# A seven-product 2x2 block form for the down projections of a two-layer decoder step, with the hidden rows in three parts

## The reference

```
h  = rmsnorm(x)                         # 1032 x 1024
u  = h @ W_up                           # 1024 -> 2 * 2816, float32
u  = u[t-2]*w[0] + u[t-1]*w[1] + u[t]*w[2]   # causal, per column, with a saved state
z  = silu(u[:, :2816]) * u[:, 2816:]
x  = x + z @ W_down                     # 2816 -> 1024
```

## Time and profile before

| | us |
|---|---|
| median of 3 runs | 2892.84 |
| the profiled execution: span | 2890.9 |
| PE busy | 2675.3 |
| DVE busy | 1348.3 |
| ACT busy | 1153.7 |
| POOL busy | 468.1 |
| up tiles 1 to 43 of layer 0 | 451.50 |
| down tiles 0 to 6 of layer 0 | 202.32 |

### The profile page before, as it was taken

The page is one execution under the profiler, slowest core; times in us unless marked ns, Lnnn a source line. Parts: engine busy times, 40 slices in busy tenths (PEclk is TensorE's granted clock), DMA queues, the critical chain, the costliest instruction groups (busy, mean ns, idle before and its releaser), DMA issues.

```text
span 2890.9 us, 47469 instructions
## 1 busy us (share of the span) xinstructions
PE 2675.3 (93%) x18103; PEld 1816.1 (63%) x18103; DVE 1348.3 (47%) x2199; ACT 1153.7 (40%) x1599; POOL 468.1 (16%) x626
## 2 busy tenths in 40 slices
PE   5898988898888798999999999999999999999997
PEld 3666676655565465666666665566655666666664
DVE  8254454315899736444444113522345444443123
ACT  4665655322777624444443112211124444442111
POOL 0321303313445300111111000011100111111000
PEclk9999999999999899999999999999999999999999
DMA  3222223364000211111112111111111111111111
GB/s 129 82 74 61 66 68 118 95 188 129 1 1 1 81 51 37 51 45 49 51 51 66 51 51 35 51 51 51 47 42 44 51 51 51 51 51 66 50 50 59
DMA packets 113484, 173.20 MB, mean 60 GB/s; under 512 B 16993, under 2 KB 83922, under 8 KB 112978
## 3 DMA queue, kind: packets, MB, share of 16 engines
q1 hardware_dynamic: 92610, 150.90, 16.2%
q0 software_dynamic: 3792, 12.58, 1.3%
q10 hardware_dynamic: 16960, 8.16, 1.0%
HBM read 161.47 MB, written 14.30 MB: 61 GB/s over the span
## 4 chain that ended last, share of the span: by engine, by line
PE 74%; DVE 14%; ACT 5%; SPq 3%; issue 3%; DMA 1%; POOL 0%; ACTq 0%; DVEq 0%; POOLq 0%
PE PS L1804 62%; ACT xT L855 2%; DVE R L1552 2%; SPq L554 2%; PE PS L1784 2%; DVE R L1222 2%; PE PS L1837 2%; SPq L557 2%; DVE R L1531 1%; PE PS L1905 1%; DVE hT L1227 1%; PE PS L2072 1%; DVE R L1216 1%; PE PS L2003 1%; PE PS L2134 1%
## 5 line engine op out<-in xcount | busy, mean ns | idle before, releaser
L1804 PE MATMUL PS<-hT,R 128*128 128x344 f16 x10152 | 1486.6, 309 | 5.6 <-DVE R L530 4.4
L1804 PEld LDWEIGHTS PS<-hT,R 128*128 128x128 f16 x10152 | 993.4, 98 | 496.3 <-DVE R L530 3.4
L530 DVE SCALAR_TENSOR_TENSOR R<-W,R 128x1024 f16<-128x1024 f32 (+1 forms) x186 | 248.4, 1336 | 962.1 <-ACT R L524 961.5
L524 ACT ACTIVATE R<-W 128x1024 f16<-128x1024 f32 (+1 forms) x186 | 206.5, 1110 | 922.4 <-PE PS L1804 918.2
L1804 PE MATMUL PS<-R 128*128 128x344 f16 x3276 | 478.2, 309 | 0.0
L1804 PEld LDWEIGHTS PS<-R 128*128 128x128 f16 x3276 | 320.6, 98 | 157.2
L1700 DVE SCALAR_TENSOR_TENSOR R<-R 128x1024 f32<-128x1024 f32 x96 | 123.3, 1284 | 79.5 <-ACT R L1165 78.3
L855 ACT ACTIVATE xT<-xT 64x1024 f32<-64x1024 f32 x64 | 124.7, 1949 | 55.1 <-DMA xT<-cmp_t 54.0
L755 POOL COPY R<-R 128x2 f32 x88 | 19.2, 218 | 743.9 <-ACT R L1164 743.9
L761 POOL TENSOR_TENSOR R<-R 128x1032 f32 x44 | 94.2, 2142 | 275.3 <-ACT R L1171 275.3
L1702 DVE SCALAR_TENSOR_TENSOR R<-R 128x1024 f32<-128x1024 f32 x96 | 123.4, 1285 | 13.6 <-DVE R L1701 12.3
(11 more groups left out here) (300 smaller groups left out, 2792.7 us busy)
## 6 DMA issues: line engine op xcount, KB each, us to landing
W<-wk SPq DMA_DIRECT2D x154, 512.0 KB, 3.4
W<-wdn SPq DMA_DIRECT2D x32, 704.0 KB, 4.1
xT<-cmp_t SPq DMA_DIRECT2D x256, 64.0 KB, 1.9
xT<-x SPq DMA_DIRECT2D x16, 516.0 KB, 7.4
o_y<-hT SPq DMA_DIRECT2D x6, 688.0 KB, 3.5
o_win_s<-state_win POOLq DMA_DIRECT2D x1, 4088.0 KB, 23.8
R<-s_hgrn POOLq DMA_DIRECT2D x4, 512.0 KB, 5.6
o_hgrn_s<-R ACTq DMA_DIRECT2D x4, 512.0 KB, 3.2
```

Source lines behind the costliest of these rows:

```text
L524: act.activation(to[:, n, 0, 0:width], W[:, n, 0:width], ACT.Copy, scale=UNIT).then_inc(wh_here, 1)
L530: dve.scalar_tensor_tensor(to[:, n, 1, 0:width], W[:, n, 0:width], UNIT, to[:, n, 0, 0:width], ALU.mult, ALU.subtract).then_inc(w_split, 1)
L1804: ins = pe.matmul(wide(u)[:, m, :], weights[half], src[:, other, m * TW:(m + 1) * TW], start=(first and half == other == 0), stop=(last an ...
```

## The change

The down product z @ W_down is computed as a 2x2 block product in a form with seven products instead of eight (Winograd's variant of Strassen's). The blocks are: two output rows of 128 features (a "pair" j of output tiles), two hidden rows of 128 features (even and odd), and two halves of the columns, 516 each (`HT`). Four sums of weight blocks and four of hidden blocks are made in float32 and split into halves like everything else. Product 0 (`E1`) is copied out by ACT and added to three of the four outputs by POOL; the other products are accumulated in PSUM in part (products 1, 3 and 5 in one place, 0 and 2, 4 and 6 in two others) and read by DVE six times. Each product is row pairs x 6 matmuls of 258 columns.

The hidden rows are no longer all kept. They come in three parts: rows 0 to 5, 6 to 13 and 14 to 21 (`FIRST`, `PAIRS`), each followed by its pairs. Between the last up tile that a part needs and its pairs stands the spare row 6 or 14 (parts 0 and 1). In part 2 output tiles 6 and 7 are made in the plain form with 72 matmuls each; so there are 4, 4 and 3 pairs. Tile 7 is the tile in thirds. The squares for the norm are taken in part 2. Loops over up tiles on ACT, DVE, POOL and SP become written-out lists; PE keeps its loops for the up tiles.

The order of the work and PE's and DVE's part of one pair:

```diff
+def ffn_order():
+    order = []
+    for part, (start, stop) in enumerate(((0, 7), (7, 15), (15, 22))):
+        order += [("up", k) for k in range(2 * start, 2 * stop)]
+        if part < 2:
+            order += [("pair", part, j) for j in range(KD // 2)]
+    return order + [("tile", 6)] + [("pair", 2, j) for j in range(3)] + [("tile", 7)]
...
+            def pair(layer, item, first):
+                s, part = PAIR[layer, item], item[1]
...
+                for n, (moving, which) in enumerate(((0, 0), (5, 1), (2, 0), (7, 1), (4, 2), (6, 1), (3, 2))):
+                    if n == 0 and s:
+                        pe.wait_ge(product_read, 6 * s - 4)
+                    if n == 1:
+                        if s:
+                            pe.wait_ge(product_read, 6 * s - 1)
+                        if first:
+                            wait_emptied(pe, units[0])
+                    if n == 2:
+                        pe.wait_ge(e1_here, s + 1)
+                    if n == 3:
+                        pe.wait_ge(product_read, 6 * s + 1)
...
+                    if n == 5:
+                        pe.wait_ge(product_read, 6 * s + 3)
+                    if n == 6:
+                        pe.wait_ge(product_read, 6 * s + 4)
+                    pe.wait_ge(block_low, BLOCKS * s + n + 1)
+                    out = accumulator(part, which)
+                    for q in range(PAIRS[part]):
+                        if first:
+                            need = {0: 1, 5: 3, 2: 2, 7: 4, 4: 3, 6: 3, 3: 2}[moving]
+                            pe.wait_ge(z_here, 4 * (q0 + q) + need)
+                        rows = ZC[:, q, :, moving * HT:(moving + 1) * HT]
+                        for half, others in ((0, (0, 1)), (1, (0,))):
+                            for m in range(2):
+                                for other in others:
+                                    ins = pe.matmul(out[:, m, :], WB[:, n, half, q * P:(q + 1) * P],
+                                                    rows[:, other, m * HW:(m + 1) * HW],
...
+            def pair_turn(layer, norm, item, after, second):      # on DVE
...
+                dve.wait_ge(e1_added, 3 * s + 1)
+                read(1, t, 1, 1)
+                if after[0] == "pair":
+                    sums(layer, after, range(3))
+                    blocks_low(layer, after, range(1))
+                else:
+                    split_low(dve, STEP[layer, after])
+                read(2, t, 0, 0)
...
+                if part == 2 and j:
+                    square_added(2 * j - 1, norm)
+                dve.wait_ge(e1_added, 3 * s + 2)
+                read(3, t + 1, 1, 1)
+                if after[0] == "pair":
+                    blocks_low(layer, after, range(2, 3))
+                    sums(layer, after, range(3, 4))
```

ACT's part of a pair, and what DVE and ACT do at an odd up tile:

```diff
+            def pair_turn(layer, norm, item, after, second):      # on ACT
+                act.wait_ge(product_full, BLOCKS * s + 1)
+                if s:
+                    act.wait_ge(e1_added, 3 * s)
+                act.activation(two(E1), accumulator(part, 0), ACT.Copy, scale=1 / UNIT).then_inc(e1_here, 1)
...
+                if after[0] == "pair":
+                    blocks_high(layer, after, range(BLOCKS))
...
+            def ffn(layer, norm, last=False):                      # on ACT, for an up tile k of hidden row h
+                    act.activation(three(U[n][:, 2:2 + TT]), wide(u + k), ACT.Copy, scale=1 / UNIT).then_inc(u_here, 1)
+                    act.activation(three(Y[n]), wide(u + k), ACT.Copy, scale=FWD[:, k:k + 1]
+                                   ).then_inc(ps_free[(u + k) % 2], 1)
+                    if after[0] == "pair":
+                        blocks_high(layer, after, range(3, BLOCKS))
+                    if n == 0:
+                        continue
+                    act.wait_ge(y_here, layer * KF + h + 1)
+                    act.activation(Y[0], Y[0], ACT.Silu).then_inc(silu_here, 1)
+                    act.wait_ge(zm_here, layer * KF + h + 1)
+                    for turn, cols in hidden_spans(h):
...
+                    if after[0] == "tile":
+                        blocks_high(layer, second, range(1, BLOCKS))
...
+            def hidden_sums(layer, h):                             # on DVE
+                b11, b12, b21, b22, t1, t2, t4 = (ZR[:, n * HT:(n + 1) * HT] for n in range(BLOCKS))
+                own.link(dve.tensor_tensor(t1, b12, b11, ALU.subtract))
+                own.link(dve.tensor_tensor(t2, b22, t1, ALU.subtract))
+                dve.tensor_tensor(t4, b21, t2, ALU.subtract).then_inc(t4_here, 1)
+                if h >= FIRST[2]:
+                    dve.wait_ge(z_here, 4 * (layer * KH + h // 2) + 1)
+                dve.tensor_tensor(b12, b22, b12, ALU.subtract).then_inc(t4_here, 1)
```

More of the change, by code:

```diff
@@ L38 @@
 KH = KF // 2
+HT = TT // 2
+HW = HT // 2
+FIRST = (0, 6, 14)
+PAIRS = (3, 4, 4)
+BLOCKS = 7
 HA = 4
@@ L114, with steps, one @@
 plan()
-WK = KF * TT
+WK = 4 * 8 * HT
 WKW = 1056
+def ffn_order():
[5 more added lines that the diff above has]
+    return order + [("tile", 6)] + [("pair", 2, j) for j in range(3)] + [("tile", 7)]
+FFN = ffn_order()
+STEP, CLASSIC, ARRIVED, PAIR = {}, [], [], {}
+def steps():
+    step, tiles, seen = 0, 0, [0, 0]
+    def one(name, whole, loads=1):
+        nonlocal step, tiles
+        STEP.setdefault(name, step)
+        CLASSIC.append(tiles)
+        tiles += whole
+        seen[step % 2] += 16 * loads
+        ARRIVED.append(seen[step % 2])
+        step += 1
+    for name, count in (("heads", HA * HEAD_TILES), ("kv", 6), ("mix_out", KD), ("ffn", 0), ("conv_in", 3 * KD),
+                        ("conv_out", KD), ("ffn", 1)):
+        if name != "ffn":
+            for _ in range(count):
+                one(name, True)
+            continue
+        for item in FFN:
+            if item[0] == "pair":
+                PAIR[count, item] = len(PAIR)
+                for _ in range(2):
+                    one((count, item), False, 2 if item[1] == 1 else 1)
+            else:
+                one((count, item), True)
+steps()
 def program(nc, x, wk8, wdn, small, cst, hmask, s_hgrn, wgate, pages, cmp_t, slc_kt, slc_v, win_kt, win_v, state_win,
@@ L1640, in sum_third, with residual_end @@
                 dve.tensor_tensor(a, a, SQ[1][:, m * TW:(m + 1) * TW], ALU.add).then_inc(acc_here if m == TN - 1 else acc_third, 1)
[L1642 to L1652 removed]
+            def residual_end(norm, v):
                 add_third_of(norm, 0, v)
@@ L2180, in whole @@
                             ready(f)
-                        ins = product(u + k, [W2H[:, k % 2, half, f * P:(f + 1) * P] for half in range(2)], src[:, f],
+                        ins = product(u + k, [W2H[:, k % 2, half, f * P:(f + 1) * P] for half in range(2)], src(f),
                                       f == 0, f == KD - 1)
@@ L2240, in _ @@
-            stage("mix_out", H2, after=1,
-                  ready=lambda f: pe.wait_ge(*((mix_a, f + 1) if f < HA else (mix_b, f - HA + 1))))
-            stage("up0", H2, before=1)
-            down("down0", 0, 2)
-            stage("conv_in", H2, before=2)
-            stage("conv_out", Z2, after=3, ready=lambda f: pe.wait_ge(cy_here, f + 2))
-            stage("up1", H2, before=3)
-            down("down1", KF, 4)
+                    last_tile(u + 2 * pairs - 1, c + 2 * pairs - 1, src, after)
@@ L2248, in _ @@
+            stage("mix_out", lambda f: H2[:, f], after=1,
+                  ready=lambda f: pe.wait_ge(*((mix_a, f + 1) if f < HA else (mix_b, f - HA + 1))))
+            ffn(0, 1, 2)
+            stage("conv_in", lambda f: H2[:, f], before=2)
+            stage("conv_out", hidden_row, after=3, ready=lambda f: pe.wait_ge(cy_here, f + 2))
+            ffn(1, 3, 4)
             mean_third(4, TN - 1)
```

608 lines of the change are left out of this document (391 added, 217 removed).

## The result

The changed kernel takes 2900.39 us (median of 7 runs, 2899.99 to 2907.81) where the kernel before takes 2892.67 in the same series: a ratio of 1.0036, 95% interval [1.0025, 1.0046]. It is slower by 7.7 us; 2902.4 was forecast. Its profiled execution took 2907.81 us, span 2906.0, the longest of its seven.

The account below looks back on a forecast made before the run. PE was taken as the bound, busy for 93% of the span with 74% of the chain. Twice +20.1 us a layer, less 30.6, gave +9.6: span 2900.5, median 2902.4 us, range 2874 to 2924.

Parts of the forecast that it names:

- E1: Third part: PE waits for ACT's copy of product 0, queued behind a high half; 1.0 us a layer.
- case A: Whole kernel: the summed forecast holds, 2902.4 us, slower by 0.33%; own range 2888 to 2922; chance 0.55.
- What is removed: Down projection up to the last tile: shorter matmuls take 195.3 us for 202.3, -7.0 a layer.
- Rival D: In the pairs, short matmuls do not shrink but stay near 0.125 us each: +50, 2953 us; chance 0.05.
- The clock: After PE idles, matmuls run for a while at clock 0.50: 4.4 us a layer, bounds 0 and 8.
- The entries: First pairs of parts 0 and 1: PE waits for product 0's copy, behind DVE's spare-row product; 5.2 and 5.1 us.
- sign of being wrong: First pair: ACT copies product 0 within 3 us of it; or all pairs take much over 185 + 20 us.
- Part 2: Third part, no spare row in front: five PE waits adding to 9.6 us a layer, bounds 4 and 13.
- The other reading: POOL beside DVE: both run at a reduced rate, no exclusive lock; third part's POOL waits about halve, 2896 us.
- Rival B: Covers hold: POOL and DVE do not exclude each other, slow stretches hide; -13.8 in all, 2879 us; chance 0.22.
- C: DVE bounds the pairs: weights land 2 us later, its third read late in all 22; +44, 2945 us; chance 0.1.
- E: Part entries: only half of each wait before product 0's copy is seen, 5 for 5.1 + 5.1; 2892 us; chance 0.08.

Follow-up runs that it names:

- the last kernel: Changed kernel with weight blocks split earlier in all parts, product 0 copied first, the spare row's product and last up tile's taps moved later: 2861.45 us, 0.9895 of before.
- the control: The changed kernel run again with no edit, as reference for the other follow-ups: 2903.78 us, 1.0040 of the kernel before.

## Why the prediction was right

It was right in sign and size, 2902.4 for 2900.39, and case A held. By its own steps, in us a layer:

| step | predicted | measured, layer 0 / 1 |
|---|---|---|
| what is removed, up to the last tile | -7.0 | -4.9 / -4.7 |
| entry of part 0; of part 1 | 5.2; 5.1 | 4.84; 4.06 |
| exits | 1.9 | 2.12 |
| inside the pairs | 0.9 | 0.4 |
| part 2 | 9.6 | 10.7 / 9.5 |
| clock | 4.4 | 6.5 / 6.2 |
| stage, without the wait before the last tile | +20.1 | +23.8 / +22.4 |
| norm transition, that wait included | -14.9 | -15.3 |
| end, that wait included | -15.7 | -17.0 |

**What is removed** was over-sized by 2.1. The last kernel gives it without the clock's part: 648.97 us of PE for 653.82, -4.9. Its 672 matmuls of part 1 take 74.34 us, 0.1106 each, where the step took 0.110, and the 504 of part 0 take 56.5 in their four groups, 0.112 each; over all 1680 such differences make 2.0 us. Rival D (0.125) is ruled out.

**The clock** was under-sized by 2. The same 4848 matmuls keep PE busy for 655.50 us in the changed kernel and 648.97 in the last one, so half clock costs 6.5 us. The step took one stretch for each entry, 3.4 us a layer, and hid most of part 2's beside DVE, 1.0. By the same comparison the entries cost 4.4 and 4.0, part 2 2.1 and 2.2. The waits it lies behind can be short: in layer 1 the clock is 0.50 from 2822.00 to 2824.00, behind the wait of 2.48 us, which agrees with the 2.15 of the earlier trace rows. In layer 0 the clock behind the same wait is still 1.00 (1743.73 to 1746.00) and falls to 0.50 behind the next one, of 3.56. So the length of one wait does not tell whether the clock falls.

**The entries**: the mechanism is as told. ACT's own wait ends with the DVE product of row 6:

```profile
1262.89 1.23 DVE L2005 TENSOR_TENSOR R<-R 128x1032 f32<-128x1032 f32 x1
...
1264.15 0.60 ACT L1294 ACTIVATE R<-PS 128x516 f32<-128x516 f32 x1 [3.49 <-DVE R L2005]
```

In part 1 the forecast put the blocks prepared a tile earlier in the way; they were mostly not, 1.0 less. What the forecast did not see is how little the named cause was worth: with that wait removed the time did not fall, and with E1 copied at once the stage stayed. Its sentence "Queued behind that mult on DVE are all reads of the pair" held half of the answer; the other half is what POOL's additions do to whatever stands there. Neither sign of being wrong came: ACT starts to copy E1 6.4 us behind product 0 (18 matmuls from 1255.82), and the pairs together take 210.9 and 209.5 us, for 185 + 20.

**Part 2**: five waits at the five places named. Single ones are off (2.43, 1.90, 0.31, 2.48, 3.56 for 2.8, 2.25, 1.0, 1.5, 2.05). E1 was nearly free, read 3 too cheap. Two fetches were taken to be in after about 4 us; DVE starts on them 6.4 and 6.5 us behind the first issue, and 5.7 and 5.1 without the store of the hidden states behind them, which was not in the sum. The store is worth 0.6 and 1.4 us of the wait. Without it the fetches still come over a microsecond later than was forecast; why is open.

**POOL beside DVE** is now shown, by two edits: a DVE op of 0.68 takes 0.68 beside a POOL instruction that reads nothing, 1.16 beside pieces of 258 columns and up to 2.67 beside 1548. The Trainium skill, SBUF — State Buffer, "SBUF: two separate sides", has the lock held for a whole instruction and counts only a GpSimd op that reads SBUF against DVE's two-input ops; both halves agree with these rows. The other reading, two engines at a reduced rate, would not have let 516 columns get faster when POOL's work was cut into more pieces.

**The last tile** gave 32.3 for 30.6: the transition 41.16 for the 42.38 of the earlier trace rows, the end 32.75 where 34 to 35 was named. Of the 1.3 us that the end is better than its -15.7, 0.7 is in DVE's chain: with the wait in front it ends 29.7 us after the pairs (2902.19) for the 30.45 of the sum. Another 0.5 is in what follows it, 3.8 us for 4.3 before.

The steps add to +13.9 in the two profiled executions, whose spans differ by 15.1, and the medians by 7.7. The 4 us by which the steps were too low are not in the medians, whose profiled execution was the longest of seven. In the control's series the medians lie 11.2 apart (2903.78 and 2892.60), so the change costs some 8 to 11 us, with the forecast of 9.6 between. That the total came within 2 us is in part luck: what is removed and the clock were each some 2 us a layer too favourable, while the entry of part 1 was priced 1 too high and the gain behind the pairs 1.7 too low. Rival B would have needed the entries and part 2 covered: it takes new orders on ACT and DVE to get there (the last kernel's stage is 1.3 and 1.6 us over that of before). C did not occur (fetches at 3.6; its 44 us make 2946, not 2945), and E is refuted at 4.84 and 4.06.

## What to carry to other kernels

A form with fewer products pays nearly what it says on PE (here 23 of 25 us a layer), and the stalls at its borders decide whether anything is left; list them, and for each ask what stands in the queue of the engine that serves it, not which semaphore ends it. Taking away the named wait shortened no stage by more than 1.6 us here, twice, as the next consumer waited for the same queue; moving work that nobody waits for (weight blocks a tile earlier, taps and a row's product later), with E1 copied first, turned +0.4% into -1.05%. Where VectorE and GpSimd both read SBUF, moving one op earlier can put it under the other's lock, so the order of both has to be read together.

## What was not expected of the hardware

A VectorE op over 8 columns, 0.22 us alone, takes 1.23 when a POOL addition of 516 columns is under way. It waits 1.0 us, as long as the tap of 1024 columns beside it (2.34 for 1.28): what the lock costs goes by what POOL is doing and not by the size of the op that waits, so splitting off small ops saves nothing there. And the lock alternates: with POOL's work in pieces, DVE and POOL took strict turns, 1.16 us a DVE op, and POOL needed 12.28 us for what takes 7.0 in three instructions.
